# Two weight pieces as one 512-column operand in the token-major projections of block 1

## What is computed

```python
def first_block(x, ...):
    h = x
    for i in range(DEPTH):                                  # DEPTH = 2
        h = h + 0.5 * swiglu_ffn(rmsnorm(h, norm_ffn1[i]), w_ffn1_in[i], w_ffn1_out[i])
        u = rmsnorm(h, norm_mix[i]) @ w_mix_in[i]
        z, xbc, dt_raw, q, k, v, q_idx, k_idx, w_idx = jnp.split(u, SPLIT_POINTS, axis=-1)
        y_ssd = ssd_mixer(z, xbc, dt_raw, ...)               # 16 heads of 64, a state-space mixer
        y_att = dsa_mixer(q, k, v, q_idx, k_idx, w_idx, positions)   # 8 heads of 128
        h = h + jnp.concatenate([y_ssd, y_att], axis=-1) @ w_mix_out[i]
        h = h + 0.5 * swiglu_ffn(rmsnorm(h, norm_ffn2[i]), w_ffn2_in[i], w_ffn2_out[i])
    return rmsnorm(h, final_norm)
```

## Time and profile before

| | us |
|---|---|
| median of 3 runs | 2656.02 |
| lowest and highest | 2654.87, 2657.49 |
| the profiled execution | 2657.64 |
| its span, first to last instruction | 2655.8 |

### The profile page before, as it was taken

The page is one execution under the profiler, slowest core; times in us unless marked ns, Lnnn a source line. Parts: engine busy times, 40 slices in busy tenths (PEclk is TensorE's granted clock), DMA queues, the critical chain, the costliest instruction groups (busy, mean ns, idle before and its releaser), DMA issues.

```text
span 2655.8 us, 40458 instructions
## 1 busy us (share of the span) xinstructions
PE 2617.2 (99%) x17054; PEld 2285.5 (86%) x17054; DVE 1928.6 (73%) x2550; ACT 1278.2 (48%) x1659; POOL 594.0 (22%) x419
## 2 busy tenths in 40 slices
PE   8999999999999999999999999999999999999999
PEld 7889888888889987988898777778888899889887
DVE  7867576885876657687799655468778779865884
ACT  5445546544444545544523544544444443655543
POOL 3411010331330001132105301024303203411430
PEclk9999999999999999999999999999999999999999
DMA  7555795555555688455333322245555544434653
GB/s 245 186 192 179 245 301 165 185 186 194 190 181 177 206 269 270 159 190 194 91 96 100 85 70 64 70 142 192 188 186 191 181 120 129 122 116 147 219 182 103
DMA packets 442330, 445.57 MB, mean 168 GB/s; under 512 B 13711, under 2 KB 433672, under 8 KB 442150
## 3 DMA queue, kind: packets, MB, share of 16 engines
q1 hardware_dynamic: 438744, 436.80, 51.5%
q0 software_dynamic: 2400, 5.40, 1.0%
q10 hardware_dynamic: 1006, 0.79, 0.1%
HBM read 441.79 MB, written 1.17 MB: 167 GB/s over the span
## 4 chain that ended last, share of the span: by engine, by line
PE 90%; DVE 4%; issue 2%; ACT 2%; DMA 1%; POOL 1%; SPq 0%; ACTq 0%; DVEq 0%; POOLq 0%
PE bank L1953 31%; PE bank L1913 22%; PE bank L1957 16%; PE bank L1905 6%; PE bank L1948 4%; PE bank L2229 2%; PE bank L2468 1%; PE bank L2459 1%; PE bank L2139 1%; DVE lower L773 1%; DVE R L3235 1%; PE bank L2312 1%; DMA ring<-in_w_in 0%; PE bank L2326 0%; DMA bias_na<-rpb_scratch 0%
## 5 line engine op out<-in xcount | busy, mean ns | idle before, releaser
L1226 ACT ACTIVATE upper<-ring 128x2048 fp32r<-128x2048 f32 (+1 forms) x238 | 443.9, 1867 | 625.8 <-PE bank L1957 618.8
L2616 DVE TENSOR_TENSOR lower<-ring,upper 128x2048 fp32r<-128x2048 f32 (+1 forms) x238 | 596.0, 2505 | 190.2 <-ACT upper L1226 189.9
L1953 PE MATMUL bank<-h_pair,upper 128*128 128x512 f32 x2464 | 606.5, 393 | 10.8 <-DVE h_pair L2633 5.9
L1953 PEld LDWEIGHTS bank<-h_pair,upper 128*128 128x128 f32 x2464 | 455.8, 189 | 102.0 <-issue 11.7
L1957 PE MATMUL bank<-h_pair,lower 128*128 128x256 f32 x2464 | 339.7, 284 | 0.0
L1913 PE MATMUL bank<-h_up,lower 128*128 128x512 f32 (+1 forms) x1280 | 337.5, 346 | 0.7 <-DVE h_low L2683 0.7
L1957 PEld LDWEIGHTS bank<-h_pair,lower 128*128 128x128 f32 x2464 | 325.6, 192 | 11.4
L1953 PE MATMUL bank<-hid_pair,upper 128*128 128x512 f32 x1232 | 297.4, 392 | 0.0
L980 POOL TENSOR_TENSOR A<-A 128x512 f32<-128x512 f32 x77 | 209.4, 2719 | 334.5 <-ACT A L1275 334.5
L1913 PEld LDWEIGHTS bank<-h_up,lower 128*128 128x128 f32 x1280 | 223.6, 189 | 46.3 <-issue 17.3
L1953 PEld LDWEIGHTS bank<-hid_pair,upper 128*128 128x128 f32 x1232 | 225.7, 188 | 43.2
(11 more groups left out here) (377 smaller groups left out, 4291.6 us busy)
## 6 DMA issues: line engine op xcount, KB each, us to landing
ring<-in_w_ffn_in SPq DMA_DIRECT2D x154, 1024.0 KB, 5.1
ring<-in_w_ffn_out SPq DMA_DIRECT2D x56, 1024.0 KB, 4.9
ring<-in_w_mix_in SPq DMA_DIRECT2D x48, 1024.0 KB, 5.4
ring<-in_w_mod SPq DMA_DIRECT2D x48, 1024.0 KB, 7.4
ring<-in_w_in SPq DMA_DIRECT2D x42, 1024.0 KB, 5.3
ring<-in_w_ffn_out SPq DMA_DIRECT2D x28, 768.0 KB, 4.2
ring<-in_w_mix_out SPq DMA_DIRECT2D x16, 1024.0 KB, 5.5
ring<-in_w_in SPq DMA_DIRECT2D x16, 512.0 KB, 4.6
```

Source lines behind the costliest of these rows:

```text
L1226: act.activation(f.upper(p)[:, 0:n], slot[:, 0:n], ACT.Copy).then_inc(up_ready, 1)
L1953: pe.matmul(bank[:, 0:2 * T], up[:, cols], x_pair.rearrange("p e t -> p (e t)"), start=first, stop=False)
L2616: dve.tensor_tensor(f.lower(p)[:, 0:n], slot[:, 0:n], f.upper(p)[:, 0:n].bitcast(F32), ALU.subtract)\
```

## The change

Pieces of qidx and qkv are used in pairs. An item is now one half of the tokens (128) times both pieces, 512 columns in one matmul, 24 matmuls; the next item is the other half with the same two pieces. So both pieces have to be there and split before the first item of the pair, and both hold their places in the ring and their uppers until the second has ended. ACT takes an item out with one instruction (`take_half`).

```diff
-            def form1_a(it, w, cols):
-                bank = start_item(it)
-                up, low = w
-                for s in range(2):
-                    o, tokens = bank[0][:, cols * s:cols * (s + 1)], slice(128 * s, 128 * (s + 1))
-                    for k in range(KD):
-                        c = slice(k * cols, (k + 1) * cols)
-                        for n, (x_, w_) in enumerate(((h_up, up), (h_low, up), (h_up, low))):
-                            mm = pe.matmul(o, x_[:, k, tokens], w_[:, c], start=k == 0 and n == 0,
-                                           stop=k == KD - 1 and n == 2)
+            def form1_a(it, first, s):
+                bank = start_item(it)[0]
+                a, b = PIECES[first], PIECES[first + 1]
+                pe.wait_ge(low1_ready, b.n + 1)
+                tokens = slice(128 * s, 128 * (s + 1))
+                for k in range(KD):
+                    at_a, at_b = [UPPER_HALVES[p.up][k // 4] + PC * (k % 4) for p in (a, b)]
+                    up = two_at(over_uppers, whole, at_a, at_b)
+                    low = two_at(over_ring, NW * SLOT, a.slot * SLOT + PC * k, b.slot * SLOT + PC * k)
+                    for n, (x_, w_) in enumerate(((h_up, up), (h_low, up), (h_up, low))):
+                        mm = pe.matmul(bank[:, :], x_[:, k, tokens], w_, start=k == 0 and n == 0, stop=k == KD - 1 and n == 2)
```

The tables that say what stands where:

```diff
-MOD_AT = [("logit", u) for u in (0, 1, 3, 4, 6, 7)] + [("head", i) for i in range(SSD_H)] + [("unit", 0), ("unit", 1)]
-LAST_TURN_AT = ("unit", 3)
+MOD_AT = [("logit", u) for u in (0, 1, 3, 6, 7)] + [("head", i) for i in (0, 3, 4, 5) + tuple(range(7, SSD_H))] + \
+    [("unit", u) for u in (0, 0, 1, 2, 3, 3)]
+LAST_TURN_AT = ("unit", 4)
+QKV_SPLIT_AT = [("z", 2), ("z", 3), ("logit", 3), ("logit", 5)] + [("head", i) for i in (0, 1, 2, 4, 5, 6, 10, 10)]
+QKV_AHEAD, MIXO_AFTER = 2.5, ("mod", 15)
...
+QIDX_UPPERS = ((2, 3), (1, 2))
+Z_UPPERS = ((0, 1, 2, 0), (0, 3, 1, 0))
+QKV_UPPERS = (5, 3, 1, 2, 6, 7, 1, 2, 6, 7, 1, 2)
```

More of the change, by code:

```diff
@@ L101, in mix_fills @@
             fills.append(("qkv", QKV_AT.index(slot)))
[L102 to L106, removed]
+        for n in range(MOD_PIECES):
+            if MOD_AT[n] == slot:
+                fills.append(("mod", n))
+                if n >= 4 and n % 4 == 1:
+                    fills.append(("turn", n // 4 - 1))
         if slot == LAST_TURN_AT:
@@ L135, in layer_pieces @@
             if name != "dkT":
-                out.append((name, i, item))
+                out.append((name, i, item + 1 - i if name == "qidx" else item))
             item += 1
[L138 to L144, removed]
+    item_of = {fill: item + n for n, fill in enumerate(fill for fills in FILLS.values() for fill in fills)}
+    item += len(item_of)
+    queued = []
+    for (what, i), at in item_of.items():
+        if what == "mod":
+            queued.append((at, what, i, at))
+        elif what == "qkv":
+            queued.append((item_of[what, i // 2 * 2] - QKV_AHEAD + 0.1 * (i % 2), what, i, item_of[what, i | 1]))
+    queued.append((item_of[MIXO_AFTER] + 0.05, "mix_out", 0, item))
+    out += [piece for _, *piece in sorted(queued)]
+    for i in range(1, MIX_OUT_PIECES):
         out.append(("mix_out", i, item + i))
@@ L167, in fill_tables @@
             item += 1
[L168 to L172, removed]
+    assert item == MIXO_ITEM
+    return item_of, {(name, i): n for n, (name, i, _) in enumerate(LAYER1) if name in ("qkv", "mod", "mix_out")}
 FILL_ITEM, FILL_PIECE = fill_tables()
-assert FILL_ITEM["turn", 4] > FILL_ITEM["mod", 19] > FILL_ITEM["turn", 3] + 1
+YS_ITEM = max(FILL_ITEM[fill] for slot, fills in FILLS.items() for fill in fills
+              if slot[0] == "logit" or slot[0] == "head" and slot[1] < SSD_H - 2)
+YS_TURN = min(n for (what, n), item in FILL_ITEM.items() if what == "turn" and item > YS_ITEM)
+assert FILL_ITEM["turn", YS_TURN - 1] + 1 < YS_ITEM or (FILL_ITEM["turn", YS_TURN - 1] - YS_ITEM) % 2
 FF2_ITEM, FF2_PIECE = MIXO_ITEM + MIX_OUT_PIECES, MIXO_PIECE + MIX_OUT_PIECES
@@ L321, in plan_pieces @@
     out, held, uses, mixed, mixed1 = [], {}, [0] * NW, 0, 0
-    up_held, turn = {}, 0
+    up_held, released = {}, list(range(-NW, 0))
     def add(name, i, layer, end, slot):
@@ L2983, in qkv_ahead @@
                 def qkv_ahead(kind, i):
-                    for what, n in FILLS.get((kind, i), ()):
-                        if what == "qkv" and n + 1 < len(QKV_AT):
-                            split1_low(dve, poss + FILL_PIECE[what, n + 1])
+                    for n in range(len(QKV_SPLIT_AT)):
+                        if QKV_SPLIT_AT[n] == (kind, i):
+                            split1_low(dve, poss + FILL_PIECE["qkv", n])
                 def turned_mod(kind, i):
```

118 lines of the change are left out of this document (77 added, 41 removed).

## The result

The changed kernel takes 2688.11 us (median of 4 runs, 2682.97 to 2689.11) against 2655.44 us for the kernel before in the same job: 1.0119 times as long, 95% interval 1.0107 to 1.0131. It is slower by 32.7 us, where 11 were forecast. Its profiled execution has a span of 2685.6 us, 29.8 more than before's 2655.8.

The account below looks back on a forecast made before the run. The prediction took PE, busy 99% of the span, to bound the kernel. Width -9.0, new waits +16.4 and clock +3.4 gave +10.8 us on the 2656.0 median: 2667 us predicted, range 2655 to 2675.

Parts of the forecast that it names:

- The width: Token-major items, 28 in both layers: 24 matmuls of 512 columns take 5.44 us against 5.76, 9.0 us saved.
- places 1 to 4: New PE waits a layer: qidx 1.6 us, z loop and first logits 3.45, first turn 1.8, load burst 1.3.
- What it moves: Four mod items and one turn go from heads to attention units: counted as nothing, bounds 0 to -2.2 us a layer.
- The clock: PE's clock falls to half once a layer behind logit 2, some 3.4 us long: 1.7 us lost, 3.4 in both.
- place 2: z loop and first logits: PE waits 1.85 us for the Relu, then 1.6 for a lower, 3.45 a layer.
- The sum: Whole kernel: -9.0 + 16.4 + 3.4 = +10.8 us, 2666.8 us on the median.
- more waits, or a second fall: Rival: late pair loads at qkv 6 or 8, or clock fall at first turn; 1.5 to 4 us a layer; chance 0.14.
- place 3: First turn, now at head 0: DVE reads it behind pair 1's segment sums, so qkv 4 waits 1.8 us a layer.
- The clock holds: Rival: four short matmuls between the waits at the first logits keep the clock up; 2663.4 us; chance 0.22.
- the wide matmul saves nothing: Rival: in token-major items 512 columns take 0.240 us, as two of 256; 2675.8 us; chance 0.03.
- faster: Rival: products moved to the attention units fill existing PE waits, 2.2 us a layer; 2649.6 to 2652.8 us; chance 0.07.
- The signs to look for: In the trace: items of 5.4 to 5.5 us, named PE waits, PE's matmul time about 9 us less, waits some 16 more.

Follow-up runs that it names:

- the kernel with four places taken back: Changed kernel with last turn read early, qkv 0 and 1 splits earlier, second qidx split earlier, turn 0 read ahead of pair 1's segments: 2653.87 us.
- the narrow forms: Changed kernel, and the kernel with four places taken back, each 512-column product issued as two of 256 columns: 2697.04 us and 2666.12 us.
- the last kernel: The kernel with four places taken back, plus ACT's unit 0-3 modulation copies first and second-layer DVE eviction of convolution item 5 before the subtraction: 2651.81 us.
- two small places: Changed kernel with second qidx weight copied and subtracted earlier, and turn 0 read ahead of pair 1's segments: 2681.47 us.

## Why the prediction was right or wrong

The direction was right and the size was wrong by a factor of three.

- **The width**: the step between starts was right (0.68 us for three), the term was too large: 5.6 us on the items, not 9.0. It took the step for the whole item. The items behind row products gained only 0.1 us. Against the kernel before, the items of the kernel with four places taken back are 6.4 us shorter.
- **The pairs, places 1 to 4**: right, one by one. 17.1 us measured in the list, 16.4 predicted; each wait had the releaser named. Taking them back gave the same sizes, with the clock's share.
- **What it moves**: this is the step that failed, and most of the miss: 18.5 us, where the measured loss and the forecast one are 22 apart. It took "nothing" for the moved products and turns, with bounds of 0 to -2.2 us a layer, none above zero. It looked for shared banks at mod 20 and mod 22, found 1.4 us each and stopped there. The same look at the next items of the same run (turn 5, mixer-output product 0, product 1) would have shown product 1 on the pair of turn 5, and DVE's read behind the subtraction for weight 2. LAST_TURN_AT is one line of the diff and cost 18.5 us: 12.5 of wait, and 4.2 of the rest half clock. For mods 20 and 22 the waits came, 0.7 and 1.2 us, less than the 1.4 counted. By `MOD_AT` the units gain four products and a turn as it says, but three of the products come from the heads and one product and one turn from the logits. From the last qkv item to mixer-output product 0 the first layer takes 25.2 us where it took 19.1: 6.1 more, of which 1.5 are added waits for ACT's copies.
- **The clock**: place 2 made it fall in each layer, as forecast, but for 6.8 us in the first layer and 3.4 in the second, which cost 2.7 and 1.5 us, not 1.7 each. The new place made it fall again: 8.4 us in all against 3.4.
- **The sum**: predicted -9.0 + 16.4 + 3.4 = 10.8. Measured, from the rows above: -5.6 + 17.1 + 12.5 + 8.4, and 3.0 for ACT's copies at the units (3.7 less the 0.7 that the kernel before had of the kind), makes 35.4. The spans differ by 29.8. Of the 5.6 between them, 2.3 are waits of the kernel before at its line L1948 (2.0 on a lower half, now 0.9, and 1.7 on DVE's R, now 0.5), 0.6 its own waits at product 1, and 1.5 a stretch of half clock that it had at 2240 us and the changed one had not. Another 1.6 are in the items: by the starts the 28 took 169.9 us before and take 166.9 now, 4.2 of it half clock, so they are 7.2 us shorter and not 5.6. The modulation products and turns take 1.1 us less by the starts (0.5 a layer, inside the prediction's bound), the row products 1.1 more, and other waits 0.7 more. No run isolates these small ones.
- **The rivals**: "more waits, or a second fall" was nearest (2670 to 2675), but it looked for them at late loads of pairs and for the fall at place 3. "The clock holds", "the wide matmul saves nothing" and "faster" are out. The range ended at 2675 since no case in it added more than 4 us a layer to the forecast, and the wait at product 1 with its half clock was 8.1 us in the first layer and 8.6 in the second.
- **The signs to look for**: PE's matmul time was not 9 us less (2617.0 against 2617.2), since matmuls at half clock are longer and count as busy. That sign was badly chosen; the starts of matmuls at full clock show the width.

## What to carry to other kernels

When a schedule moves an item whose buffers rotate in pairs, list for every item behind it who held its pair before and where in that engine's program the releasing read stands, for all of the stage and not only for the item that moved; one item more or less swaps the pairs of all that follow. A read of a third of a microsecond that frees a pair belongs at the head of its engine's step, ahead of work that waits for a third engine: here that was worth 18.5 us in one place and 16 in another. Where one engine is the bound and its clock falls behind waits, price a wait with the clock behind it (here a third to 60% more at the two places where it fell in both layers), and measure a width by the starts of instructions, not by busy time.

## What the runs showed of the hardware

- **The clock's fall is not decided by one wait's length.** In the second layer PE waits for mod 13's load in most of these kernels. The clock was at half behind waits of 1.95 us (last turn moved), 2.31 and 2.37 (the narrow forms), 2.42 (qkv splits earlier) and 2.61 us (the last kernel). It stayed at 1.00 behind 1.86 us (two small places), 1.92 us (all four taken back) and 2.57 us, the last in the changed kernel itself. The wait of 2.18 us at qidx 0 in the second layer made it fall in four kernels and not in three. The two waits of place 2 (1.77 and mostly 1.60 us), with four short matmuls between, made it fall in every kernel that had them, and in the one with the two small places taken back it was already at half between them. Single waits of 1.68 us, and of 1.67, never did. The first row is the changed kernel behind its 2.57 us, the second the kernel with the last turn moved behind its 1.95 us; the clock is the third number from the end:

```profile
1035.50:1039.00 3.50, 3.47 (x29) 2.30 (x30) 3.43 (x10) 0.39 (x1) 0.00 (x0) 1.00 1.10 348
...
1028.00:1031.40 3.40, 3.40 (x23) 2.13 (x24) 3.33 (x10) 0.38 (x1) 0.00 (x0) 0.50 1.10 348
```

- **VectorE's mask products take twice as long while GpSimd works.** In the kernel with one product moved to head 6, the mask product of 128x256, with two inputs in SBUF, takes 1.01 us where it takes 0.48 elsewhere, under a stretch in which GpSimd is busy for 3.34 of 3.5 us; the segments, which read a bank, keep their 0.47 beside it. Not every product with two inputs in SBUF is slowed as much: the one of line L3119 takes 0.48 us at 360.85, under GpSimd's work, where it takes 0.42 without.

```profile
355.50:359.00 3.50, 1.53 (x14) 0.30 (x2) 3.46 (x6) 0.39 (x1) 3.34 (x6) 1.00 1.10 360
...
358.96 0.47 DVE L3174 TENSOR_SCALAR A<-bank,small 128x256 f32<-128x256 f32 x1
```

The four mask products of that stretch took 3.2 us from first start to the segments, and the four segments behind them 1.3, so they made the late read of turn 2 later by some 1.9 us (an estimate from these two). The Trainium skill, GPSIMD Engine Reference, section "1. Specifications", says that GpSimd's SBUF interfaces are shared with VectorE, with contention for VectorE's instructions that have two SBUF inputs; for the mask products the trace agrees, with the 1.01 us above.
